# Decode-row compressions of a hybrid decoder step on one core: row 0 between the mLSTM state updates in two halves, the other rows one place earlier

## What is computed

```
sub = rows.reshape(B, n_sub, CMP_STRIDE, NSA_KV_HEADS, 2, HEAD_DIM)
for r in range(R):                       # R = 2
    hid = hid + einsum('bnshcd,csde->bnhce', sub[:, r:r + n_cmp],
                       w1[:, r * CMP_STRIDE:(r + 1) * CMP_STRIDE])
kv = einsum('bnhce,ced->bnhcd', gelu(hid), w2)
```

## Time and profile before

| | us |
|---|---|
| median of 3 runs | 1544.53 |
| lowest, highest | 1539.28, 1557.38 |
| the profiled execution | 1540.57 |
| its span, first to last instruction | 1538.9 |
| PE busy | 1410.1 (92%) |
| DVE busy | 808.5 (53%) |
| ACT busy | 406.2 (26%) |

### The profile page before, as it was taken

The page is one execution under the profiler, slowest core; times in us unless marked ns, Lnnn a source line. Parts: engine busy times, 40 slices in busy tenths (PEclk is TensorE's granted clock), DMA queues, the critical chain, the costliest instruction groups (busy, mean ns, idle before and its releaser), DMA issues.

```text
span 1538.9 us, 27976 instructions
## 1 busy us (share of the span) xinstructions
PE 1410.1 (92%) x9816; PEld 1009.3 (66%) x9816; DVE 808.5 (53%) x2032; ACT 406.2 (26%) x787; POOL 168.6 (11%) x312
## 2 busy tenths in 40 slices
PE   5998999999899999898999899998989999989895
PEld 3673877888775576464558368777888746755542
DVE  1354555765545844862125365476655466567610
ACT  4230100321122153651431201031112121536400
POOL 0000000000000063520000000000000002726000
PEclk9987899999789999899999779899976899979998
DMA  7131331231004164784232324124100131755701
GB/s 318 70 112 55 120 130 56 83 112 56 1 1 170 50 177 134 225 290 160 103 147 61 106 89 147 59 61 144 56 2 1 59 150 56 204 175 154 301 1 68
DMA packets 92928, 171.73 MB, mean 112 GB/s; under 512 B 14081, under 2 KB 79794, under 8 KB 86898
## 3 DMA queue, kind: packets, MB, share of 16 engines
q1 hardware_dynamic: 79778, 120.39, 23.4%
q0 software_dynamic: 13008, 49.54, 9.2%
HBM read 157.08 MB, written 21.12 MB: 116 GB/s over the span
## 4 chain that ended last, share of the span: by engine, by line
PE 74%; DVE 12%; issue 8%; ACT 3%; DMA 1%; SPq 0%; POOL 0%; DVEq 0%; POOLq 0%; ACTq 0%
PE bank L581 16%; PE bank L618 13%; PE bank L1186 8%; PE bank L2785 4%; PE bank L514 2%; PE bank L1212 2%; PE bank L1320 2%; PE bank L814 2%; PE bank L2275 1%; DVE area L1707 1%; DVE area L1672 1%; PE bank L1308 1%; PE bank L822 1%; PE bank L1297 1%; PE bank L584 1%
## 5 line engine op out<-in xcount | busy, mean ns | idle before, releaser
L581 PE MATMUL bank<-stream,hT 128*128 128x512 f32 (+3 forms) x768 | 263.2, 500 | 0.5 <-DVE hT L451 0.5
L618 PE MATMUL bank<-hT,stream 128*128 128x272 f32 x960 | 234.3, 407 | 5.1 <-DVE area L1560 5.1
L618 PEld LDWEIGHTS bank<-hT,stream 128*128 128x128 f32 x960 | 189.0, 198 | 46.3 <-DVE area L1560 5.3
L581 PEld LDWEIGHTS bank<-stream,hT 128*128 128x128 f32 x768 | 147.1, 195 | 100.7 <-issue 86.9
L1186 PE MATMUL bank<-stream,prm 128*128 128x256 f32 x512 | 126.9, 411 | 0.4 <-DVE YT L1541 0.4
L2785 PE MATMUL bank<-stream,YT 128*128 128x512 f32 x256 | 112.5, 601 | 5.6 <-DVE YT L2693 5.6
L1186 PEld LDWEIGHTS bank<-stream,prm 128*128 128x128 f32 x512 | 105.4, 208 | 18.0 <-issue 1.4
L2785 PEld LDWEIGHTS bank<-stream,YT 128*128 128x128 f32 x256 | 49.0, 193 | 66.5 <-issue 60.5
L407 POOL DMA_DIRECT2D stream<-in_slcK x128 | 69.0, 549 | 169.2 <-PE bank L584 135.5
L407 POOL DMA_DIRECT2D stream<-in_slcV x128 | 68.5, 539 | 84.6 <-PE bank L2239 41.1
L2801 DVE TENSOR_TENSOR X<-bank,X 128x512 f32<-128x512 f32 x16 | 11.1, 692 | 100.5 <-PE bank L2785 100.5
(11 more groups left out here) (630 smaller groups left out, 2313.4 us busy)
## 6 DMA issues: line engine op xcount, KB each, us to landing
stream<-in_cmpL SPq DMA_DIRECT2D x256, 128.0 KB, 2.3
stream<-in_win_ SPq DMA_DIRECT2D x12, 2048.0 KB, 7.3
stream<-in_slcK SPq DMA_DIRECT2D x128, 64.0 KB, 2.3
stream<-in_slcK POOLq DMA_DIRECT2D x128, 64.0 KB, 2.5
stream<-in_slcV SPq DMA_DIRECT2D x128, 64.0 KB, 2.6
stream<-in_slcV POOLq DMA_DIRECT2D x128, 64.0 KB, 2.7
stream<-in_wout SPq DMA_DIRECT2D x4, 2048.0 KB, 11.1
out_winpast<-in_winraw POOLq DMA_DIRECT2D x2, 4064.0 KB, 26.0
```

The lines of the kernel that those rows point to most:

```text
L581: last = nc.tensor.matmul(ps[:, 0:w], hT[:, k, tok(i)], ws[:, k, :], start=(k == 0), stop=(k == KT - 1))
L618: last = nc.tensor.matmul(ps[:, 0:HALF], ws[:, k, 128 * f:128 * f + 128], hT[:, k, HALF * s:HALF * s + HALF], start=(k == 0), stop=(k == K ...
```

## The change

The eight compressions of decode rows keep their matmuls but change places. Row 0 is done in two halves (c = 0 in front of the update of head 1, c = 1 in front of that of head 3), into one bank, and DVE reads it behind the clearing of HIDD, ahead of the heads. Head h takes row h + 1. The RWKV phase takes rows 5 and 6, block 1 row 7, block 0 none. In the order of loads row 4 now comes before F1 and F2. The first tokens' memory projection is cut too: its first four matmuls move ahead of the cumulated gates (in front of the wait for LF), the other four stay.

```diff
-            items += [("w", l, n) for n in ("T0", "F0", "T1")] + [("wmem", l)] + [("cmp", l, b) for b in range(4)]
-            items += [("w", l, n) for n in ("F1", "F2")] + [("cmp", l, b) for b in range(4, DB)]
+            items += [("w", l, n) for n in ("T0", "F0", "T1")] + [("wmem", l)] + [("cmp", l, b) for b in range(5)]
+            items += [("w", l, n) for n in ("F1", "F2")] + [("cmp", l, b) for b in range(5, DB)]
...
-        def pe_memkv(pe, l, i):
+        def pe_memkv(pe, l, i, ks=range(KT)):
...
-            ps = pe.open("mk", l, i)
-            for k in range(KT):
+            ps = bank("mk", l, i) if ks[0] else pe.open("mk", l, i)
+            for k in ks:
                 last = nc.tensor.matmul(ps[:, :], HM[:, k, 128 * i:128 * i + 128], w[:, k, :], start=(k == 0), stop=(k == KT - 1))
+            if ks[-1] < KT - 1:
+                return
...
             pe.full(last.then_inc(pe_done, 1), "qn", l)
+            pe_memkv(pe, l, 0, range(4))
...
-            pe_memkv(pe, l, 0)
+            pe_memkv(pe, l, 0, range(4, KT))
...
             for h in range(NH):
                 hs = slice(64 * (h % 2), 64 * (h % 2) + 64)
+                if h % 2:
+                    pe_compress(pe, l, 0, (h // 2,))
                 pe.wait_ge(dve_done, at("VXe", l, h))
...
-                pe_compress(pe, l, h)
+                pe_compress(pe, l, h + 1)
                 pe.wait_ge(dve_done, at("PJ", l, h))
...
             dve(nc.vector.memset(HIDD, 0.0).then_inc(dve_done, 1))
+            dve_compress(dve, l, 0)
...
                 dve.name("PJ", l, h)
-                dve_compress(dve, l, h)
+                dve_compress(dve, l, h + 1)
...
-            pe_compress(pe, l, 4)
+            pe_compress(pe, l, 5)
             pe.wait_ge(dve_done, at("LW", l))
             pe_project_rows(pe, l, "F2", 2)
-            pe_compress(pe, l, 5)
+            pe_compress(pe, l, 6)
...
-        def pe_compress(pe, l, b):
+        def pe_compress(pe, l, b, parts=(0, 1)):
...
-            ps = pe.open("ab", l, b)
-            for c in range(2):
+            ps = bank("ab", l, b) if parts[0] else pe.open("ab", l, b)
+            for c in parts:
                 for j in range(8):
                     last = nc.tensor.matmul(ps[:, 256 * c:256 * c + 256], w1p[:, c, j, :], cs[:, :, j, c, :], start=(j == 0), stop=(j == 7))
-            pe.full(last.then_inc(pe_done, 1), "ab", l, b)
-            pe.name("used", "cmp", l, b)
+            if parts[-1]:
+                pe.full(last.then_inc(pe_done, 1), "ab", l, b)
+                pe.name("used", "cmp", l, b)
...
-                if lev == 3 and m < 2:
-                    pe_compress(pe, l, 6 + m)
+                if lev == 3 and m == 1:
+                    pe_compress(pe, l, 7)
```

More of the change, by code:

```diff
@@ L1546, in dve_r @@
                     dve(nc.vector.tensor_scalar(AG, AG, 0.5, 0.5, ALU.mult, ALU.add).then_inc(dve_done, 1))
-                    dve_compress(dve, l, 4)
+                    dve_compress(dve, l, 5)
                     dve_r_front(dve, l, 0, 0)
@@ L1585, in dve_r @@
             dve.name("fm", l, 0)
-            dve_compress(dve, l, 5)
+            dve_compress(dve, l, 6)
             for m in range(4):
@@ L1720, in dve_r_block @@
                 elif lev == 3:
-                    if m < 2:
-                        dve_compress(dve, l, 6 + m)
+                    if m == 1:
+                        dve_compress(dve, l, 7)
                     dve_r_ahead(dve, l, m + 1, 4)
```

## The result

| | before | after |
|---|---|---|
| median | 1539.28 (9 runs) | 1560.05 (9 runs) |
| lowest to highest | 1531.06 to 1560.17 | 1541.16 to 1575.17 |
| profiled execution, span | 1538.9 | 1560.7 |
| mean granted clock, that execution | 0.915 | 0.902 |

The ratio is 1.0112 (95% interval 1.0072 to 1.0152): the changed kernel is about 1% slower, where I had forecast 1539.4 us and at most 1557. Ratios, intervals and the means further down leave out the executions that ran more than 1.5% above the fastest one of the same kernel.

The account below looks back on a forecast made before the run. PE's own order was taken to bound the kernel, with gains only where PE waited or ran slowly. Terms -5.2 + 4.5 - 1.9 + 1.0 gave -1.6 us a layer, 1537.4, plus 2.0 for the median: 1539.4 us; range 1528 to 1557.

Parts of the forecast that it names:

- Row 6 out of the solve: First RWKV block without row 6's compression: -6.4 us, less a clock allowance, gives -5.2 us a layer (-6.4 to -3.2).
- The allowance of 1.2 for the clock: RWKV blocks: +1.2 us a layer, between 0 and 3.2, for slower products once block 0's dense work is gone.
- The halves: Row 0 between the state updates: first half 5.6 us, second 3.45 us, +4.5 us a layer.
- (b): State updates: halves run at 1.2 GHz, deciding from 10.7 us for both; +7.8 us a layer, 1556 us; chance 0.14.
- The first head: From update 3 to the first head's values product: 16.0 us instead of 17.9, -1.9 us a layer.
- The memory split: Memory projection in two halves, the first ahead of L740: +1.0 us a layer (-0.3 to +4.5).
- The sum: Whole kernel: four local terms add to -1.6 us a layer, -3.2 us for two, giving 1539.4 us.
- (a): Whole layer: the clock stays up, -6.3 us a layer, -12.6 in all, 1528 us; chance 0.18.
- (c): RWKV block: its wait goes to another chain, nothing gained there; +3.6 us a layer, 1548 us; chance 0.06.

Follow-up runs that it names:

- row6_eighth: The kernel before, with row 6's compression in RWKV block 0 cut to an eighth and the rest of its products left out: ratio 0.9929.
- row0_added: The kernel before, plus row 0's two halves between the state updates as extra work, into a bank nobody reads: ratio 1.0154.
- row0_eighth: The changed kernel, with row 0's two halves between the state updates cut to an eighth each: ratio 1.0004 to the kernel before.
- the solve halves: The kernel before, rows 6, 7 halved into the solve's waits: ratio 0.9855; likewise rows 5, 6, 7 in blocks 0 to 2, row 4 in the head: 0.9805.
- The delays: The kernel before plus extra 2-column matmuls: four or eight a layer ahead of F1, ratios 1.0068 and 1.0092; 16 behind both RWKV stages, 1.0023.

## Why the prediction was wrong

**Row 6 out of the solve (-5.2 a layer).** The gain without the clock, -6.4, was near: -5.6 and -6.0 in the profile from group to group, -10.9 us for seven eighths of it in two layers at equal clock. The allowance of 1.2 for the clock was mis-sized for the changed kernel: behind L1335 it cost 3.5 us at once in layer 0, and the next block 2.9 and 3.9 us more (37.2 to 40.1 and 41.2). I had capped it at 3.2 in all. In row6_eighth the clock over the whole run came out the same (L 269 and 269).

**The halves (+4.5).** Too low by a third in place: +6.9 and +5.3 us in the changed kernel, +4.9 and +7.4 in row0_added, 12 us for two layers and not 9. The first half took 6.61 and 5.67 us, against 5.6. The second came to 5.27 once, because the clock fell between the halves, which I had in the sum of neither the forecast nor fully of rival (b). At equal clock it is worse: 17.0 us for the halves alone. The sum had booked as gained that the dense halves bring the clock up early, and row0_added shows that this gain was lost again elsewhere.

**The first head (-1.9).** -1.8 and -0.7. PE waited 2.17 and 2.55 us for row 0's bank, and then 0.17 for DVE, as worked out. (The prediction counted from 161.27 us; the values product begins at 161.11.)

**The memory split (+1.0).** In the changed kernel +2.1 and -0.6 up to the products behind it (L764), +2.2 and +1.1 up to the first state update, +1.5 a layer at equal clock. As a local sum right; yet alone it cost 1.1%.

**The sum, which is the step that failed.** It adds the terms of four places and takes the clock in the rest of the kernel as it was in one profile, a term put at nothing. At equal clock the parts do add up: row 6 -12.5 (eight sevenths of -10.9), the halves with the first head +15.5 (the change less row0_eighth), the split +3, together +6, where the change has +5.3 to +6.5. Nothing is left over for the order of the rows and loads. The forecast had -10.4, +5.2 and +2 for these three, so the mis-sized term among them is the halves, by 10 us. The other 10 us of +15.9 are about 24 us more of low clock at 0.425, most of it in the RWKV stages (65 and 85 us at 1.2 GHz in the profile, against 37 and 65), of which all instructions but one compression are unchanged. The view that would have warned me was there: the kernel before has the same stage twice, at 153.9 and 165.5 us, and its nine runs spread by 2%. A kernel whose identical stages differ by 12 us has no term that can be trusted to 2 us by itself.

**The rivals.** (b) had the side right and the place only in part. By its own mark, 10.7 us for both halves, it held in layer 0 (11.9) and not in layer 1 (9.4), and the larger part of the loss lay 150 us behind the halves. (a) was seen in the solve halves, not in this change. (c) falls with row6_eighth. The times given for the three leave out the 2.0 us that the forecast adds for the median; with them they are 1530, 1558 and 1550, and the result is above all of them.

**What stays open.** The delays show that a small shift ahead of the RWKV stages costs more than its length, in low clock, and that the same matmuls behind them do nothing of the kind. That the memory split and row 0's halves lose by the same route is argued from their equal-clock figures and from the low clock of the stages in single profiles; no run holds the entry time fixed while splitting. What in a shift makes the clock stay low longer is not shown, nor why the kernel before sits at a good point.

## What to carry to other kernels

Before adding up local terms, look whether identical stages of the kernel, and its repeated runs, differ by more than the terms; if so, read the granted clock by stage, and time every small shift instead of forecasting it. Put dense filling into waits that are about as long as a piece of it, cut to fit, in the stage whose clock falls: two halves in 2.35 and 0.85 us of waiting, in place of a whole row beside them, gave 1.5%; two halves around 0.84 us waits, where no row had been, lost about 1%.

## What was not expected of the hardware

A delay of 1 us a layer made the kernel 0.7% slower (0.2 to 1.1%), all but 2 us of it in low clock, while four times as many matmuls in one piece near the end cost 0.2% (-0.1 to 0.6%). The same RWKV stage, 1471 to 1473 recorded matmul instructions, took from 153.9 us at a mean clock of 0.88 to 172.4 us at 0.76, and in one and the same unedited layer 165.5 us in one execution and 154.0 in another. Over repeated runs of one kernel, 1 us more at 1.2 GHz went with 0.42 us more of time.
